# Two-layer recurrent and attention decoder step on one core: first loads in order of use, slabs in halves, and one y tile ahead of the gate products

## What is computed

```python
y = jax.nn.gelu(x @ w_y + b_y, approximate=True)
u = x @ w_x + b_x
upad = jnp.concatenate([conv_buf.astype(u.dtype), u], axis=1)
xc = conv_b + sum(conv_w[k] * upad[:, k:k + T] for k in range(CONV_W))
r = jax.nn.sigmoid(jnp.einsum('btni,nij->btnj', xb, w_ga) + b_ga).reshape(B, T, D_RNN)
gi = jax.nn.sigmoid(jnp.einsum('btni,nij->btnj', xb, w_gi) + b_gi).reshape(B, T, D_RNN)
log_a = -LRU_C * r.astype(jnp.float32) * jax.nn.softplus(-lam.astype(jnp.float32))
...
out = (h.astype(x.dtype) * y) @ w_out + b_out
```

## Time and profile before

| what | value |
|---|---|
| median of 3 runs | 1093.65 us (1092.61 to 1093.67) |
| the profiled execution, its time | 1092.76 us |
| its span (first to last instruction) | 1091.0 us |
| TensorE busy | 1075.5 us, 99% |
| VectorE busy | 800.2 us, 73% |
| ScalarE busy | 561.4 us, 51% |
| granted TensorE clock, mean | 0.995 of full |

### The profile page before, as it was taken

How to read it: one execution, slowest core, us unless ns; L and a number is a source line. 1 busy time by engine, 2 the same in 40 slices (tenths; PEclk the granted TensorE clock), 3 DMA queues, 4 the chain that set the end, 5 groups by cost and what they waited for, 6 DMA issues and landing times.

```text
span 1091.0 us, 22309 instructions
## 1 busy us (share of the span) xinstructions
PE 1075.5 (99%) x8535; PEld 1054.4 (97%) x8535; DVE 800.2 (73%) x1277; ACT 561.4 (51%) x995; POOL 142.5 (13%) x187
## 2 busy tenths in 40 slices
PE   8999999999999999999999999999999999999996
PEld 8999999999999999999999878999999999999996
DVE  6999999896858668565864673889958668586666
ACT  5999857562423524233666775675532514325233
POOL 2111031000000000012244564300000000000023
PEclk9999999999999999999999999999999999999998
DMA  7323305041323403262141220230422413224202
GB/s 251 114 88 97 110 27 155 1 145 39 128 71 103 135 27 127 74 232 86 35 122 45 79 60 21 59 98 2 154 84 92 135 37 117 83 90 136 78 2 83
DMA packets 63709, 98.66 MB, mean 90 GB/s; under 512 B 4384, under 2 KB 44768, under 8 KB 63616
## 3 DMA queue, kind: packets, MB, share of 16 engines
q1 hardware_dynamic: 62944, 94.81, 27.4%
q0 software_dynamic: 400, 2.21, 0.6%
q10 hardware_dynamic: 288, 0.59, 0.1%
HBM read 95.06 MB, written 3.56 MB: 90 GB/s over the span
## 4 chain that ended last, share of the span: by engine, by line
PE 88%; DVE 6%; ACT 3%; issue 1%; DMA 1%; SPq 0%; POOL 0%; DVEq 0%; ACTq 0%
PE bank L1920 12%; PE bank L1921 11%; PE bank L1922 11%; PE bank L2165 8%; PE bank L2167 8%; PE bank L2166 8%; PE bank L2139 6%; PE bank L2141 6%; PE bank L2140 6%; PE bank L1998 2%; PE bank L2000 2%; PE bank L1999 2%; PE bank L2274 1%; PE bank L2299 1%; PE bank L2317 1%
## 5 line engine op out<-in xcount | busy, mean ns | idle before, releaser
L1114 DVE TENSOR_TENSOR w_lo<-stage,w_hi 128x1024 fp32r<-128x1024 f32 x120 | 144.9, 1220 | 55.9 <-ACT w_hi L648 55.9
L648 ACT ACTIVATE w_hi<-stage 128x1024 fp32r<-128x1024 f32 x120 | 124.3, 1054 | 113.6 <-DVE stage L1132 64.2
L1920 PE MATMUL bank<-x_hi,w_hi 128*128 128x288 f32 (+1 forms) x560 | 163.9, 293 | 0.8 <-DVE w_lo L1107 0.7
L1921 PE MATMUL bank<-m_lo,w_hi 128*128 128x288 f32 (+1 forms) x560 | 162.2, 290 | 0.0
L1921 PE MATMUL bank<-x_lo,w_hi 128*128 128x288 f32 (+1 forms) x560 | 161.7, 289 | 0.0
L1920 PE MATMUL bank<-m_hi,w_hi 128*128 128x288 f32 (+1 forms) x560 | 161.6, 289 | 0.0
L1922 PE MATMUL bank<-m_hi,w_lo 128*128 128x288 f32 (+1 forms) x560 | 161.6, 289 | 0.0
L1922 PE MATMUL bank<-x_hi,w_lo 128*128 128x288 f32 (+1 forms) x560 | 160.9, 287 | 0.0
L2139 PE MATMUL bank<-m_hi,w_hi 128*128 128x288 f32 (+1 forms) x512 | 147.7, 289 | 0.3 <-DVE m_lo L1468 0.3
L2141 PE MATMUL bank<-m_hi,w_lo 128*128 128x288 f32 (+1 forms) x512 | 147.6, 288 | 0.0
L2140 PE MATMUL bank<-m_lo,w_hi 128*128 128x288 f32 (+1 forms) x512 | 147.4, 288 | 0.0
(11 more groups left out here) (270 smaller groups left out, 2770.4 us busy)
## 6 DMA issues: line engine op xcount, KB each, us to landing
stage<-w_up SPq DMA_DIRECT2D x64, 512.0 KB, 4.4
stage<-w_down SPq DMA_DIRECT2D x64, 512.0 KB, 3.7
stage<-w_qkv SPq DMA_DIRECT2D x10, 512.0 KB, 3.8
stage<-w_x SPq DMA_DIRECT2D x8, 512.0 KB, 6.1
stage<-w_y SPq DMA_DIRECT2D x8, 512.0 KB, 3.4
stage<-w_out SPq DMA_DIRECT2D x8, 512.0 KB, 3.6
stage<-w_o SPq DMA_DIRECT2D x8, 512.0 KB, 4.0
y_t<-acc SPq DMA_DIRECT2D x4, 288.0 KB, 2.4
```

The costliest lines, as they stand in the source:

```text
L648: A(hi, raw, ACT.Copy).then_inc(s_whi, 1)
L1114: vt.tensor_tensor(lo, raw, hi.bitcast(F32), ALU.subtract).then_inc(s_wlo, 1)
L1920: mm(out, wh, xh, start=(k == 0), stop=False)
L1921: mm(out, wh, xl, start=False, stop=False)
```

## The change

The first loads are issued in the order in which they are used, and the two w_x slabs of pair 0 in halves, each half with its own split on ScalarE and VectorE. The w_y slabs and the second half of x are issued only when earlier pieces have landed. The sample tokens come in the same rows as the second half of x. TensorE's y tiles of step 0 and x tiles of step 1 go slab by slab and piece by piece instead of waiting for all. The vectors are asked for after the third piece of x instead of the first. `derive_series` moves from before the x split of the second half to behind `gate_lo`. 11 constant products instead of 13 are made at the start. In steps 1 to 6 the first y tile comes ahead of `gates(s - 1)`; in step 7 the gate products keep their place.

```diff
-WARM = 13
+WARM = 11
...
+        def gates_done(s, g=4):
+
+            return mark[("gate", s)] + g + (s < 6)
...
+            def load_half(j, part):
+
+                st = where[j][0]
+                k0 = 4 * j + 2 * part
+                sp.dma_start(stage[:, st, 512 * part:512 * part + 512].rearrange("p (k c) -> p k c", k=2),
+                             xv[:, k0:k0 + 2, 0:256]).then_inc(s_arrived[st] if part else s_early[j], 16)
+
+            def load_xb(k):
+                sp.dma_start(acc[:, 2 * k:2 * k + 2, 256:TOK],
+                             x_b[256 * k:256 * k + 256, :].rearrange("(k p) t -> p k t", p=128))\
+                    .then_inc(s_xb[k], 16)
 
             load_x(0)
-            load(0, xv[:, 0:4, 0:256])
-            for k in (1, 2):
-                load_x(k)
-            load(1, xv[:, 4:8, 0:256])
+            load_half(0, 0)
+            load_x(1)
+            load_half(0, 1)
+            load_x(2)
+            load_half(1, 0)
+            sp.wait_ge(s_xa[0], 16)
             load_x(3)
-            load_pair(("pair", 0), yv, 0, 2)
+            load_half(1, 1)
+            sp.wait_ge(s_xa[1], 16)
+            load(2, yv[:, 0:4, 0:256])
+            sp.wait_ge(s_xa[2], 16)
+            load(3, yv[:, 4:8, 0:256])
+            sp.wait_ge(s_xa[3], 16)
+            for k in range(4):
+                load_xb(k)
             for p in range(4):
-                if p == 0:
-                    sp.dma_start(acc[:, :, 256:512],
-                                 xp_t[:, 256:512].rearrange("(k p) t -> p k t", p=128)).then_inc(s_xb, 16)
-                    sp.dma_start(acc[:, :, 512:TOK], xs_t.rearrange("(k p) t -> p k t", p=128)).then_inc(s_xb, 16)
-                else:
+                if p:
                     load_pair(("pair", p), xv, 256 * p)
...
-            x_split(0, [0])
             late = VEC["sinks"][0]
-            act.dma_start(vecs[:, 0:late], vec[:, 0:late]).then_inc(s_vec, 16)
-            split([0])
-            x_split(0, [1, 2])
-            split([1])
-            x_split(0, [3])
+            for k in range(4):
+                x_split(0, [k])
+                if k == 2:
+                    act.dma_start(vecs[:, 0:late], vec[:, 0:late]).then_inc(s_vec, 16)
+                split_half(k // 2, k % 2)
             split([2, 3])
...
                 for t in range(2):
                     m = 2 * p + t
-                    A(th_r[:, t, :n], unit(m0 + 2 * t)[:, :n], ACT.Tanh, bias=dv[:, 0, m:m + 1], scale=0.5)\
+                    act.wait_ge(s_unit, gates_done(s, 2 * t + 1))
+                    A(th_r[:, t, :n], bank[:, bank_of(m0 + 2 * t), :n], ACT.Tanh, bias=dv[:, 0, m:m + 1], scale=0.5)\
...
             dve.wait_ge(s_vec, 16)
             derive_in()
-            derive_series()
             for s in range(8):
...
                     conv_lo(0)
                     split([4])
+                    derive_series()
                     derive()
...
-                if s:
+                if s == 7:
+                    gates(6)
+                if s == 0:
+
+                    def pieces2(t):
+                        return [(*slab(w0 + 2, k // 4, 256 * (k % 4) + 128 * t), *act_cols(x_hi, x_lo, k, 0))
+                                for k in range(KT)]
+
+                    group_by_k([mark[("y", 0)] + t for t in range(2)], 0, pieces2, lambda k: ((s_wlo, j + 3 + k // 4),))
+                    continue
+                pe.wait_ge(s_wlo, j + 4)
+                pair_unit(mark[("y", s)], w0 + 2, 0, h)
+                if 0 < s < 7:
                     gates(s - 1)
-                pe.wait_ge(s_wlo, j + 4)
-                for t in range(2):
-                    pair_unit(mark[("y", s)] + t, w0 + 2, t, h)
+                pair_unit(mark[("y", s)] + 1, w0 + 2, 1, h)
```

More of the change, by code:

```diff
@@ L73, with build @@
 STAGES = 4
-WARM = 13
+WARM = 11
 SLOTS = 8
 BANKS = 8
-def build(nc, xp_t, xs_t, vec, w_y, w_x, w_ga, w_gi, w_out, w_qkv, w_o, w_up, w_down,
+def build(nc, x_a, x_b, vec, w_y, w_x, w_ga, w_gi, w_out, w_qkv, w_o, w_up, w_down,
           ck_t, cache_k, cache_v, y_t, small, k_p, v_p, k_s, v_s):
@@ L182, in build @@
         s_xa = [sem(f"x_half_a_loaded_{k}") for k in range(4)]
-        s_xb = sem("x_half_b_loaded")
+        s_xb = [sem(f"x_half_b_loaded_{k}") for k in range(4)]
+        s_early = [sem(f"first_half_of_slab_{k}_arrived") for k in range(2)]
+        s_halfhi, s_halflo = sem("half_slab_hi_done"), sem("half_slab_lo_done")
         s_arrived = [sem(f"slab_arrived_{i}") for i in range(STAGES)]
@@ L635, in split @@
                     if kind == "g" and j >= 14:
-                        act.wait_ge(s_unit, mark[("gate", 2 * ((j - 4) // 5) - 3)] + 4)
+                        act.wait_ge(s_unit, gates_done(2 * ((j - 4) // 5) - 3))
                     A(hi, raw, ACT.Copy).then_inc(s_whi, 1)
@@ L763, in _ @@
                 if s >= 1:
-                    act.wait_ge(s_unit, mark[("gate", s - 1)] + 4)
+                    act.wait_ge(s_unit, gates_done(s - 1))
                 A(xc_hi[:, :, :n], xc[s % 2][:, :, :n], ACT.Copy).then_inc(s_xchi, 1)
@@ L1186, in _, with split_half @@
             vt.memset(tiny[:, 7, :], 0.0).then_inc(s_hlo, 2)
[L1187 to L1191, removed]
+            def split_half(j, part):
+                hi, lo, raw = split_targets(j)
+                at = slice(512 * part, 512 * part + 512)
+                dve.wait_ge(*((s_whi, j + 1) if part else (s_halfhi, j + 1)))
+                vt.tensor_tensor(lo[:, at], raw[:, at], hi[:, at].bitcast(F32), ALU.subtract)\
+                    .then_inc(s_wlo if part else s_halflo, 1)
+            for k in range(4):
+                x_split(0, [k])
+                split_half(k // 2, k % 2)
             split([2, 3])
@@ L1290, in conv_lo @@
                 if s:
-                    dve.wait_ge(s_unit, mark[("gate", s - 1)] + 4)
+                    dve.wait_ge(s_unit, gates_done(s - 1))
                 vt.tensor_tensor(xc_lo[:, :, :n], xc[s % 2][:, :, :n], xc_hi[:, :, :n].bitcast(F32), ALU.subtract)\
@@ L2030, in _, with pieces1 @@
                     group_by_k(range(2), 0, pieces0,
-                               lambda k: ((s_xlo, k // 2 + 1), (s_wlo, k // 4 + 1)))
-                else:
-                    if s == 1:
-                        pe.wait_ge(s_xlo, 8)
+                               lambda k: ((s_xlo, k // 2 + 1), (s_wlo if k % 4 > 1 else s_halflo, k // 4 + 1)))
+                elif s == 1:
+                    def pieces1(t):
+                        return [(*slab(w0, k // 4, 256 * (k % 4) + 128 * t), *act_cols(x_hi, x_lo, k, 1))
+                                for k in range(KT)]
+                    group_by_k([mark[("x", 1)] + t for t in range(2)], 1, pieces1, lambda k: ((s_xlo, 5 + k // 2),))
+                else:
                     pe.wait_ge(s_wlo, j + 2)
```

18 lines of the change are left out of this document (13 added, 5 removed).

## The result

The changed kernel takes 1096.28 us (median of 8 runs, 1095.48 to 1097.93), the kernel before in the same comparison 1093.52 us (8 runs). The ratio is 1.0032, 95% interval 1.0023 to 1.0041: slower by 2.8 us on the medians, by 3.5 us on the ratio. The forecast was 1095.7, in a range of 1093.8 to 1097.6. The profiled execution took 1097.72 us.

What follows compares the result with a forecast made beforehand. The prediction took the closed chain of ScalarE and VectorE through the steps, not TensorE, as the bound up to 127.59 us. Its terms on that chain summed to +2.1 us, from 1093.65 to 1095.7 us, range 1093.8 to 1097.6.

Steps and rivals of the forecast that it cites:

- Start, chain -0.6: Loads at the start: vectors asked for later let the w_y slabs land earlier, so ScalarE and VectorE start 0.6 us earlier.
- Start, TensorE -2.0: Step 0: TensorE starts the y tiles at some 13.4 us instead of 15.41, 2.0 us earlier.
- derive_series, +1.2: Six VectorE instructions moved behind gate_lo have no idle time to cover them, making ScalarE and VectorE 1.2 us later.
- y tile 0 ahead: Step 2: TensorE stalls 2.0 us for the bank gelu of step 1 reads, losing its lead; no stall in step 1.
- Gates behind it: Gate products come later, so ScalarE waits: +0.55 us in step 1's gates, +0.5 in step 2's, smaller amounts in later steps.
- GpSimd, +0.2: GpSimd's six scale instructions move beside the x split of the second half and slow it by 0.2 us.
- rival 4: Slower by more: each of four x splits waits for a GpSimd instruction, 2.0 us instead of 0.2; 1097.5 us, chance 0.07.
- End: Output product's last slab comes 1.9 us later than at 127.59, and all 1.9 us reach the program's end.
- The signs I named: Changed profile: stalls before y tiles near 41, 69 and 97 us, ScalarE idle before th_r, output product near 129.5.
- Rival 2: Faster: TensorE keeps its 2.0 us lead and loses the 0.56 us stall at the end; 1091.1 us, chance 0.05.
- Rival 3: The order costs nothing as ScalarE's tanh has room; only derive_series and the landing stay, +0.6 us, 1094.3, chance 0.08.

Runs made afterwards that it cites:

- d: Changed kernel with gate products ahead of the y tiles again and derive_series at its old place, leaving only the new loading; 1093.35 us, ratio 1.0000.
- e: d without the four waits that hold back SyncE's loads of the w_y slabs and the second half of x; 1093.66 us, ratio 1.0006.
- f: e with the vectors asked for after the first piece of x instead of the third; 1093.16 us, ratio 1.0003.
- c: Kernel before with only the first y tile ahead of the gate products in steps 1 to 6; 1096.42 us, ratio 1.0035.
- a: Changed kernel with derive_series back at its old place, nothing else undone; 1095.18 us, ratio 1.0019.
- g: Kernel before with only derive_series moved, to behind the split of the gate weights; 1093.79 us, ratio 1.0010.
- b: Changed kernel with the gate products ahead of both y tiles again in all steps; 1094.21 us, ratio 1.0008.
- changed kernel again: The changed kernel run once more, unchanged; 1095.81 us.
- h: Kernel before with the first y tile ahead of the gate products in steps 1, 3 and 5 only; 1095.39 us, ratio 1.0020.

## Why the prediction was right, and where it wasn't

**The bound** was read rightly. O - X is 103.92 to 103.96 us in all five profiles with the old order and the old series (before twice, d, e, f), whatever the loads and however early TensorE starts. ScalarE and VectorE set O, and TensorE's lead is waited away.

**Start, chain -0.6: the mis-sized term.** It measured about +1.2 in the profiles (with GpSimd's 0.2, X is +1.4: medians 23.56 of the six profiles with the old loads, 24.96 of the eight with the new). The step that failed is "I take all of it": vectors asked for at the time of the second w_y slab were not out of its way, but moved beside it (changed kernel: asked for at 7.91, landed by 13.65, the slab taken at 14.04; the spacing of the slabs under f). So nothing was saved. And I took the rate as given, while 0.3 MB less moved in the first 8 us, 0.9 us at 353 GB/s. Holding the loads back (e) does not explain that; halves or the order of pieces are left, not told apart.

**Start, TensorE -2.0:** 1.47 at the y tiles (13.94 against a predicted 13.4), the real products from 5.86 as predicted. It was not worth nothing: it takes 1.3 us off what the new order costs in step 1 (c against a), which no term of mine had.

**derive_series, +1.2:** 1.21 alone (g), 1.26 on the new loads (b), 1.1 beside the new order (from a).

**y tile 0 ahead.** "In step 1 it does not stall, as gelu(0) is early" failed: it stalled 1.32, 1.21 and 0.66 us in the three profiles, as gelu(0) begins at 26.96. So TensorE's lead ended one step sooner than I said. In step 2 the stall is 1.87 to 1.88 against a predicted 2.0, and the tile starts at 43.15 against 41.1, the chain being later by then.

**Gates behind it.** I priced steps 2 to 6 and left out step 1, whose gates (of step 0) also go back; in c that is the largest wait of all, 2.03 us. In the changed kernel it cost little, as TensorE's earlier start leaves 0.68 us of it, and ScalarE then waits for VectorE's conv with the series anyway (38.56, 1.03 us). Behind it ScalarE waits 0.60 us in step 2 and 0.45 in step 3 (changed kernel again) where I had 0.55 and 0.5; the later waits are 0.51, 0.44 and 0.51, less the idle time that takes them up. The sum without the start and GpSimd was 1.2 + 0.55 + 0.5 - 0.25 + 0.05 + 0.55 - 0.25 + 0.15 = 2.5, and O - X grew by 2.98.

**GpSimd, +0.2:** the mean size was right, the place was not. It lay on `derive_in`: 0.46, 0.45 and 0.36 us in the profiles of the changed kernel, a and b, and nothing in the changed kernel's two repeats, d and e, 0.18 in the mean of the seven. GpSimd was done at 17.6, before the x split at 18.81. The lock of rival 4 had nothing to hold there.

**End.** "1.9 us reach the end" held in kind: what O lost went on to the end, less 0.6 us. O came 4.35 us later in the two profiles without the fall than in the two of before (means 131.71 and 127.36), and the span grew by 3.7 (1094.1 against 1090.4). From O to the last six products of TensorE 954.3 to 954.7 us pass in all fourteen profiles. Behind that, two things differ. The first is how long these six products take, 0.91 us where the granted clock is still full and 1.59 where it is half: 1.59 and 0.91 in the two profiles of before, 1.31, 0.91 and 1.59 in the three of after. It varies between executions of one kernel and is the same on both sides of the 3.7. The second is the time from the end of VectorE's last instruction to the end of the span: 3.76 to 3.86 us in the six profiles with the old loads, 3.14 to 3.24 in the eight with the new, 0.6 us less. The kernel before, then the changed one:

```profile
1082.02 1.59 PE L2430 MATMUL bank<-diag,ones 96*128 96x96 f32 x6 [1.68 <-DVE diag L1764]
...
1086.38 0.76 DVE L1777 TENSOR_SCALAR acc<-acc,vecs 128x288 f32<-128x288 f32 x2
```

```profile
1087.86 1.31 PE L2481 MATMUL bank<-diag,ones 96*128 96x96 f32 x6 [1.68 <-DVE diag L1800]
...
1091.94 0.77 DVE L1813 TENSOR_SCALAR acc<-acc,vecs 128x288 f32<-128x288 f32 x2
```

The spans end at 1091.0 and 1095.9. The diff has no edit in that part of the program; why the new loading shortens it stays open. With both, the span behind O is 962.0 to 963.4 us, so single executions move by up to 1.4 us there.

**The signs I named:** the y tile of step 2 after 40 (43.15), th_r of step 1 after 44 (48.25, and 46.74 and 46.22 without the fall), the small stalls near 69 and 97 (72.77, 100.86), O near 129.5 with a wait of 1 us (131.4 to 133.5, 0.8). All events are there, each later by the start.

So the mechanism was the predicted one, and that the number came so near (1095.7 against 1096.28) is in part luck. By the profiles the forecast was 1.8 us too low at the start and 0.5 in the gates, and 0.6 too high at the end: a span of +3.8 instead of +2.1, and +3.7 was measured without the fall. The medians of the whole times differ by only 2.8, since the two profiled executions of before (1092.76 and 1091.59) lie 1.3 us under their kernel's median, and the two of the changed kernel 0.4. Part of the +1.4 at X is therefore the choice of executions: by the ratios d, e and f, which differ from before in the loading alone, are 0.0, 0.6 and 0.3 us longer, each within about 1 us, and 0.6 more with what the end gives back. The forecast leaned to the wrong side of 0.2% (same 0.52, slower 0.44). Rival 2 (the lead survives) needed a chain 1.4 us earlier and the chain came later. Rival 3 (the order costs nothing) is refuted by c. Rival 4's price of 2.0 us at the x splits did not come.

**Open.** Why the new loads move less in their first 8 us; the upper group of h's times, 1095.4 to 1096.5, of which no profile was caught; the 0.6 us at the end of the program; and how much of the +1.4 at X all executions have, as the runs of before spread over 1091.4 to 1095.1 and g, with the old loads, has an X of 24.90.

## What to carry to other kernels

When a chain on other engines sets the point where the bottleneck engine next waits, an earlier start of that engine is worth nothing by itself, and each reorder is priced on the chain. It is worth something only where the chain waits for that engine, as here in step 1 once the gates had gone back. Find a mark behind the start and one at the end of the chain and subtract: the difference repeated within 0.04 us where the whole times spread over 3. Two marks in the middle do not see the end of the program: read the stretch behind the last mark too. When a product is moved behind another tile, list every step that reads it, the first one too, and check every bank that the moved tile takes against its reader.

## What was not expected of the hardware

The granted clock fell to half for some microseconds behind one long stall of TensorE: 1.87 us here, and also behind 2.27 us in g and 2.13 us in f. TensorE's timeline of g and its window, then those of f:

```profile
12.97 0.52 PE L1981 MATMUL bank<-x_hi,w_hi 128*128 128x256 f32 x1 [2.27 <-DVE w_lo L1107]
```

```profile
13.00:14.00 1.00, 1.00 (x5) 1.00 (x6) 0.62 (x2) 0.77 (x1) 1.00 (x2) 0.51 1.09 377
```

```profile
7.27 0.49 PE L2013 MATMUL bank<-x_hi,w_hi 128*128 128x256 f32 x1 [2.13 <-DVE w_lo L1218]
```

```profile
8.00:10.00 2.00, 2.00 (x11) 2.00 (x11) 1.39 (x3) 1.75 (x3) 0.11 (x1) 0.50 1.08 354
```

Two stalls of 1.88 us and one of 1.71 (d) had no fall behind them, so the length of the stall alone does not decide it. In f and g it cost nothing in O - X (103.96 and 105.16, as without it), as it lay ahead of X, and X stands 10.5 and 10.7 us behind the second w_y slab, where the other profiles have 10.6 to 11.1; in the changed kernel it lay on the gates and cost 1.5 us.
